# One-hot matrices begun a pair of blocks earlier, weight splits taken off GpSimd, and a gate scale moved into a copy

## What is computed

```
g_top = argmax(hf @ w_rg + b_rg)            # one of 4 groups
top_v, top_j = top_k(e_logits of that group, 2)
w_sel = softmax(top_v) * gate_g
for e in range(16):
    he = silu(hf @ w1[e]) * (hf @ w3[e])
    y = y + combine[:, e:e+1] * (he @ w2[e])
x = x + g2 * y                              # g2: the second gate, a row of 1024
```

## Time and profile before

| | us |
|---|---|
| median of 3 runs | 2121.34 (2117.25 to 2124.5) |
| the profiled execution, its own time | 2121.39 |
| its span, first to last instruction | 2119.4 |
| TensorE busy | 1874.8 (88%) |
| VectorE busy | 1388.9 (66%) |
| ScalarE busy | 950.3 (45%) |
| GpSimd busy | 145.5 (7%) |
| mean granted clock of TensorE | 0.928 of full speed |

### The profile page before, as it was taken

One profiled execution on the slowest core, in us unless ns is written; L12 is line 12 of the kernel. 1 busy time (PEld: TensorE's weight loads), 2 busy tenths in 40 slices (PEclk: granted clock), 3 DMA queues, 4 the chain that ended last, 5 costly groups with the idle time before them and its releaser, 6 DMA issues.

```text
span 2119.4 us, 31329 instructions
## 1 busy us (share of the span) xinstructions
PE 1874.8 (88%) x12399; PEld 1721.0 (81%) x12399; DVE 1388.9 (66%) x1399; ACT 950.3 (45%) x858; POOL 145.5 (7%) x156
## 2 busy tenths in 40 slices
PE   7998999989998999899998999799773788878885
PEld 7998999979997999799997999599463667667764
DVE  6445677676666454686857666758737667667765
ACT  4443656434333434466533434334223555555553
POOL 1000000000000000000000000100003211112111
PEclk9999999999998999899999999799676999989998
DMA  6554454637674555455554766333121867777773
GB/s 242 187 190 158 161 197 164 241 132 263 250 261 157 179 178 180 157 179 197 216 182 162 274 239 234 112 130 131 39 68 63 305 258 265 279 270 286 294 276 136
DMA packets 61909, 418.16 MB, mean 197 GB/s; under 512 B 7312, under 2 KB 7680, under 8 KB 13952
## 3 DMA queue, kind: packets, MB, share of 16 engines
q1 hardware_dynamic: 51392, 369.19, 47.9%
q0 software_dynamic: 10416, 47.79, 6.5%
q10 hardware_dynamic: 16, 0.01, 0.0%
HBM read 405.94 MB, written 11.02 MB: 197 GB/s over the span
## 4 chain that ended last, share of the span: by engine, by line
PE 81%; DVE 5%; issue 4%; POOL 3%; POOLq 2%; DVEq 2%; ACT 2%; DMA 1%; ACTq 0%
PE ps L1496 15%; PE ps L1498 15%; PE ps L1497 15%; PE ps L1523 5%; PE ps L1524 5%; PE ps L1527 5%; PE ps L756 3%; PE ps L757 3%; PE ps L758 3%; PE ps L740 2%; POOLq L555 1%; POOL tests L553 1%; PE ps L785 1%; PE ps L787 1%; PE ps L786 1%
## 5 line engine op out<-in xcount | busy, mean ns | idle before, releaser
L1781 DVE TENSOR_TENSOR wlo<-raw,whi 128x2048 fp32r<-128x2048 f32 x236 | 538.1, 2290 | 355.8 <-ACT whi L1630 353.0
L1496 PE MATMUL ps<-xThi,whi 128*128 128x256 f32 x2400 | 686.0, 286 | 11.2 <-DVE xTlo L1792 8.3
L1497 PE MATMUL ps<-xTlo,whi 128*128 128x256 f32 x2400 | 684.2, 285 | 0.0
L1498 PE MATMUL ps<-xThi,wlo 128*128 128x256 f32 x2400 | 684.0, 285 | 0.0
L1630 ACT ACTIVATE whi<-raw 128x2048 fp32r<-128x2048 f32 x236 | 449.9, 1910 | 380.6 <-PE ps L1498 271.5
L1496 PEld LDWEIGHTS ps<-xThi,whi 128*128 128x128 f32 x2400 | 466.0, 194 | 15.5 <-issue 11.7
L1497 PEld LDWEIGHTS ps<-xTlo,whi 128*128 128x128 f32 x2400 | 466.0, 194 | 1.8 <-issue 0.2
L1498 PEld LDWEIGHTS ps<-xThi,wlo 128*128 128x128 f32 x2400 | 465.7, 194 | 0.0
L1247 DVE TENSOR_TENSOR wlo<-raw,whi 128x2048 fp32r<-128x2048 f32 x75 | 172.7, 2309 | 24.7 <-ACT whi L917 24.4
L917 ACT ACTIVATE whi<-raw 128x2048 fp32r<-128x2048 f32 x76 | 145.6, 1917 | 48.1 <-PE ps L758 25.6
L1524 PE MATMUL ps<-wlo,hhi 128*128 128x512 f32 x352 | 137.5, 391 | 0.0
(11 more groups left out here) (418 smaller groups left out, 2792.8 us busy)
## 6 DMA issues: line engine op xcount, KB each, us to landing
raw<-stream SPq DMA_DIRECT2D x236, 1024.0 KB, 4.9
raw<-experts SPq DMA_DIRECT2D x76, 1024.0 KB, 6.8
mod<-experts SPq DMA_DIRECT2D x38, 1024.0 KB, 6.2
adaraw<-ada POOLq DMA_DIRECT2D x24, 1024.0 KB, 5.1
yd<-lnrow POOLq DMA_DIRECT2D x19, 512.0 KB, 6.8
lnrow<-ln_g POOLq DMA_DIRECT2D x6, 512.0 KB, 5.3
lnrow<-ln_b POOLq DMA_DIRECT2D x6, 512.0 KB, 6.4
x_sb<-x SPq DMA_DIRECT2D x1, 1024.0 KB, 5.1
```

The source lines that it names most:

```text
L1496: nc.tensor.matmul(outs[tile], wh, xh[:, k, :], start=k == 0, stop=False)
L1497: nc.tensor.matmul(outs[tile], wh, xl[:, k, :], start=False, stop=False)
L1498: last = nc.tensor.matmul(outs[tile], wl, xh[:, k, :], start=False, stop=k == KD - 1)
L1781: v.tensor_tensor(wlo[:, slot, :], raw[:, slot, :], whi[:, slot, :].bitcast(F32), ALU.subtract).then_inc(lo_done, 1)
```

## The change

On GpSimd the low parts of the tokens and of weight units 2 and 3 are dropped. VectorE makes them: the tokens' between `picked` and `rank_ps`, the units' behind unit 1, before the weighing. On GpSimd `one_hot(2)` follows `one_hot(1)` at once, and the loop's call is for a pair later. The wait of SyncE and TensorE on split units is now one rule. The right half of an output row is multiplied by the second gate as it is copied out of PSUM, and its multiplication at the end is left out. The left half is as before.

```diff
         def unit_split(eng, p):
-            if p == 2:
-                eng.wait_ge(ev["pool_lo"], 1)
-            elif p == 3:
-                eng.wait_ge(ev["pool_lo"], 2)
-            else:
-                eng.wait_ge(lo_done, RING + UNITS + (p + 1 if p < 2 else p - 1))
+            eng.wait_ge(lo_done, RING + UNITS + p + 1)
...
             g = nc.gpsimd
-            pool.wait_ge(ev["h2_hi"], 1)
-            g.tensor_tensor(h2split[1], cat[:, :, :], h2split[0].bitcast(F32), ALU.subtract).then_inc(ev["h2_lo"], 1)
-            for p in (2, 3):
-                pool.wait_ge(*expert_hi_done(p))
-                g.tensor_tensor(splits[p][1], raws[p], splits[p][0].bitcast(F32), ALU.subtract).then_inc(ev["pool_lo"], 1)
...
             pool.wait_ge(ev["slots"], 1)
             one_hot(1)
+            one_hot(2)
             for b in range(BLOCKS):
-                if b % 2 == 1 and b // 2 + 2 < BATCHES:
-                    one_hot(b // 2 + 2)
+                if b % 2 == 1 and b // 2 + 3 < BATCHES:
+                    one_hot(b // 2 + 3)
                 store(b)
...
             v.tensor_tensor(pick[:, 2], pick[:, 0], pick[:, 1], ALU.add).then_inc(ev["picked"], 1)
 
+            dve.wait_ge(ev["h2_hi"], 1)
+            v.tensor_tensor(h2split[1], cat[:, :, :], h2split[0].bitcast(F32), ALU.subtract).then_inc(ev["h2_lo"], 1)
+
             dve.wait_ge(ev["rank_ps"], 1)
...
-            dve.wait_ge(ev["h2_lo"], 1)
...
-            expert_lo(1)
+            for p in range(1, SPLITS):
+                expert_lo(p)
...
-                    v.tensor_copy(ybuf[:, (b - 1) % 2, 512:], bank(4)).then_inc(ev["y_right"], 1)
+                    v.tensor_tensor(ybuf[:, (b - 1) % 2, 512:], bank(4), row(mod, 5)[:, 512:], ALU.mult).then_inc(ev["y_right"], 1)
...
-                    v.tensor_tensor(lnrow[:, i, cs], lnrow[:, i, cs], row(mod, 5)[:, cs], ALU.mult)
-                    dve.drain()
+                    if half == 0:
+                        v.tensor_tensor(lnrow[:, i, cs], lnrow[:, i, cs], row(mod, 5)[:, cs], ALU.mult)
+                        dve.drain()
```

More of the change, by code:

```diff
@@ L409, in build @@
             "rw_hi rw_split routeT_ps routeT route_ps rexp_in rexp rexp2_in rexp2 "
-            "tables_in h2_hi h2_lo picked rank_ps emap slots weighed oneh0 oneh pool_lo "
+            "tables_in h2_hi h2_lo picked rank_ps emap slots weighed oneh0 oneh "
             "hT_ps y_left y_right first_w final").split()}
```

## The result

The changed kernel takes 2021.26 us at the median (2020.25 to 2022.4, 4 runs) against 2120.49 before: a ratio of 0.953, 95% interval 0.951 to 0.955. Forecast was 2014.9 with a range of 2008 to 2034. The profiled execution has a span of 2019.9 us, 99.5 less than before, and a mean granted clock of 0.948.

What follows compares the result with a forecast made beforehand. The prediction took TensorE as the bound, held up in the expert stage by waits for GpSimd's one-hot matrices. Gains of 96.7 + 8.4 + 1.4 = 106.5 us from 2121.39 gave 2014.9 us, range 2008 to 2034.

Steps and rivals of the forecast that it cites:

- The forecast case: Expert stage: TensorE's one-hot waits fall from 9 to one, rounds of 18.8 us, clock 1.00; 2014.9 us, chance 0.76.
- Waits of pairs 2 to 9: Expert stage: TensorE's waits for one-hot matrices go whole, with the lower clock around them; gain 96.7 us.
- The routing: VectorE's routing chain ahead of the experts: without GpSimd's low parts it moves 9.66 us earlier.
- The cover that was named: Routing: VectorE would next wait some 2 us for ScalarE's exponential, limiting the 12.1 us saved to 9.66.
- The tokens' low part: VectorE's subtraction of 2.29 us in its idle 2.41 us while TensorE counts ranks; cost 0, or 2.3 uncovered.
- The first matrix: `one_hot(1)` on GpSimd beside VectorE's subtractions: 0 to 2.6 us longer, taken as 1.3; TensorE's wait grows to 3.5.
- the opening: Routing up to the first one-hot matrix on GpSimd: 9.66 us gained less 1.3 us, a gain of 8.4 us.
- my worst case: Start of the stage: gain only 5.0 us, with 2.6 for the matrix and 2.3 for an uncovered subtraction.
- The scale: End of the kernel: two of four VectorE multiplications of 692 ns go; gain 1.4 us.
- 1: Expert stage: GpSimd and VectorE exclude each other, VectorE becomes the bound at 39.5 us a pair; 2030 us, chance 0.09.
- 2: Expert stage: loads become the bound; at 340 GB/s a pair takes 40.1 us, the program 2034 us; chance 0.10.
- the wrong lead: Expert stage: VectorE's low part of weights is ready 4.7 us before TensorE's first product, covering 1.3 us a pair.

Runs made afterwards that it cites:

- e1: Kernel before the change with only the one-hot matrices made a pair of blocks earlier; 2027.04 us, ratio 0.956.
- e6: Kernel of e5 with ScalarE's exponential ahead of the high parts of units 1 to 3; 2012.3 us, ratio 0.950.
- e5: Changed kernel with the one-hot matrix of pair 1 made on VectorE, from shifted slots in a new tile; 2015.25 us, ratio 0.951.
- e2: Changed kernel with the one-hot matrices and the scale put back as before, so only low parts moved to VectorE; 2112.31 us, ratio 0.997.
- e7: Changed kernel with every one-hot matrix from pair 3 on made twice on GpSimd; 2021.55 us.
- e10: Changed kernel with each output row stored twice, the second time to a further array; 2020.85 us.
- e11: Changed kernel with each output row stored three times, to two further arrays; 2022.68 us (one run).
- e12: Kernel of e6 with the shifted slots in free columns of `rt` instead of a tile of their own; 2010.99 us, ratio 0.949.

## Why the prediction was right, and where it was off

The forecast case came true: waits gone, rounds of TensorE's own length, clock 1.00. The median is 6.4 us above the forecast. Between the two profiled executions, where the steps can be followed, the gain is 99.6 us, 6.9 short of 106.5. By its steps, with shifts taken from the start of the stage:

- **Waits of pairs 2 to 9, 96.7 us.** From the first transpose to the last the stage took 427.95 us before and 331.5 now: 96.4. e1 gives 96.3 for this edit alone. Every other round is 18.88 us and not 18.82. A later matrix takes 13.9 us (1674.80 to 1688.71) to 17.7 (1712.43 to 1730.13), where 17.5 were reckoned, so it is ready long before it is wanted.
- **The routing, 9.66 us.** 9.70. The cover that was named (ScalarE's exponential) came at 2.49 us, and e6 took it away.
- **The tokens' low part, 0 us.** It is, with 0.20 us of its cover left. A few tenths more and it would have been on the path.
- **The first matrix, 1.3 us with a bound of 2.6.** This is the step that failed. The matrix took 4.0 us longer (19.7 against 15.7), and the wait grew by 2.8 us. I had let two comparisons take 4.86 us beside subtractions, since that is what they took beside two of them with a pause between; beside three in a row they took 7.58.
- **The same step left the clock out.** I had written that a wait costs more than its idle time and priced it so for pairs 2 to 9, but not for pair 1. Before, the clock had risen by then and a wait of 2.24 us didn't lower it. Now the gathers of pair 0 ran longer at the lower clock (7.56 us to the first product instead of 6.41, 1.15 more) and the longer wait brought it down again (2.16 us). So the opening gave 9.70 - 2.79 - 1.15 - 2.16 = 3.6 us where 8.4 were forecast, below the 5.0 of my worst case (whose own terms give 9.66 - 2.6 - 2.3 = 4.8). e5 brings back 7.15 us by taking the wait away.
- **The scale, 1.4 us.** From the last transpose to the end of the span it was 32.1 us and is 30.5: 1.6. No run has the scale alone; e1 and e2, which leave it at the end, have 32.0 and 32.1.
- **What lies ahead.** 2.0 us of the 6.9 are no error of a term: the profiled execution entered the stage later, in code that is the same. 3.6 + 96.4 + 1.6 - 2.0 = 99.6 us, and the spans differ by 99.5.
- **The rivals.** 1 and 2 had 0.19 of the chance and widened the range to 2034; e7, e10 and e11 show that neither was near. For VectorE I had named the wrong lead: 4.7 us for a low part of weights, where `hTlo` has 2.3 us and the pair's last `xsel_lo` only 1.25. It held, since GpSimd's work takes only tenths; that this lead was not looked at and was enough is luck.

## What to carry to other kernels

Price a wait of TensorE with the lower clock behind it, each one, the first as well; and a wait that is short enough not to lower the clock can be made one that does. Look for the smallest lead of a helper engine over all things it hands on, not for its busy share: 2.3 us of extra work cost 12 us at one place of the queue and nothing at another, with VectorE 95% busy. When work leaves GpSimd for VectorE, what stays on GpSimd slows down if VectorE's instructions now follow each other without a gap.

## What the runs showed of the hardware that was not expected

- A GpSimd comparison of 256 columns takes 1.14 us alone and up to 3.8 us beside VectorE subtractions without a gap, while VectorE loses 0.05 us to a GpSimd operation in the mean (e7); its longest subtraction there took 2.78 us (2.68 in the changed kernel) against a median of 2.29. The Trainium skill (SBUF — State Buffer, "SBUF: two separate sides") has the two exclude each other for a whole instruction. GpSimd's 2048-column subtractions did that to VectorE, for 3.8 to 4.4 us each; the short comparisons did not.
- 16 bytes more in each partition ahead of the tiles that TensorE reads made a gapless round 19.0 us instead of 18.85 (e5, e6, e12): 0.8%, all of it in the products that read `xsel`. Why is not known.
- The DMA queues moved 417 GB/s over 280 us at a share of 1.01, where a full share had looked like 367. The packets of the loads took 311 ns in the mean in the changed kernel and 282 in e11, the same loads beside three times the stores. So the share is no measure of the room that is left.
- The same code ahead of the stage took between 1595.6 and 1601.0 us in the profiled executions, so gains of 1 to 3 us are only seen in stretches of the trace.
